# Gate products of the recurrent branch on two row groups of TensorE, with four half-height tanh in place of two

## What is computed

```
xb = x.reshape(B, T, LRU_BLOCKS, LRU_BW)                  # 16 blocks of 64 features
r_gate = sigmoid(einsum('btnc,ncd->btnd', xb, w_r) + b_r)
i_gate = sigmoid(einsum('btnc,ncd->btnd', xb, w_i) + b_i)
log_a  = -8 * r_gate * softplus(-lam_param)
a      = exp(log_a)
u      = sqrt(-expm1(2 * log_a)) * (i_gate * x)
h_t    = a_t * h_(t-1) + u_t                              # a scan over time
```

## Time and profile before

| | |
|---|---|
| median of 3 runs | 2040.4 us (2035.8 to 2043.44) |
| the profiled execution | 2036.35 us, of which the span is 2034.6 us |
| PE busy | 98% of the span |
| DVE, ACT, POOL busy | 52%, 47%, 13% |
| mean granted clock of TensorE | 0.995 |
| chain of work that ended last | 82% PE, 8% ACT, 6% DVE, 2% issue |
| gate products (line 797) | 128 records, 393 ns each |
| gate tanh (line 1307) | 32, of 697 ns (`tr`) and 707 ns (`ti`) |

### The profile page before, as it was taken

One profiled execution on the slowest core, in us unless ns is written; L12 is line 12 of the kernel. 1 busy time (PEld: TensorE's weight loads), 2 busy tenths in 40 slices (PEclk: granted clock), 3 DMA queues, 4 the chain that ended last, 5 costly groups with the idle time before them and its releaser, 6 DMA issues.

```text
span 2034.6 us, 38848 instructions
## 1 busy us (share of the span) xinstructions
PE 1991.7 (98%) x15734; PEld 1944.4 (96%) x15734; DVE 1062.1 (52%) x1976; ACT 955.4 (47%) x1503; POOL 263.5 (13%) x292
## 2 busy tenths in 40 slices
PE   7999999999999999999999999999999999999997
PEld 7999999999998999999989999999999999999997
DVE  5657575755446432343457566767554374224334
ACT  5465656565236431332364757565732454213323
POOL 2312121100111200120021111120001012002100
PEclk9999999999999999999999999999999999999998
DMA  5323232222232323232313232323232323233321
GB/s 135 98 63 102 63 105 68 82 63 83 87 100 64 92 83 93 84 93 84 103 53 98 63 97 67 96 68 87 68 93 83 103 64 93 83 88 89 90 86 66
DMA packets 308456, 172.00 MB, mean 85 GB/s; under 512 B 7593, under 2 KB 303873, under 8 KB 308321
## 3 DMA queue, kind: packets, MB, share of 16 engines
q1 hardware_dynamic: 300768, 155.47, 26.4%
q0 software_dynamic: 7520, 14.59, 2.5%
q10 hardware_dynamic: 32, 0.04, 0.0%
HBM read 158.86 MB, written 11.21 MB: 84 GB/s over the span
## 4 chain that ended last, share of the span: by engine, by line
PE 82%; ACT 8%; DVE 6%; issue 2%; DMA 1%; SPq 0%; ACTq 0%; DVEq 0%
PE PJ L672 65%; PE PJ L684 4%; PE PJ L845 4%; PE PX L873 2%; ACT w_hi L1101 2%; PE PX L684 1%; PE PX L891 1%; DVE w_lo L1576 1%; PE PX L911 1%; DVE T L1687 1%; PE PX L689 1%; PE PX L927 1%; DMA w_raw<-in_w_in 1%; DVE uc L1817 1%; ACT L1318 1%
## 5 line engine op out<-in xcount | busy, mean ns | idle before, releaser
L1576 DVE TENSOR_TENSOR w_lo<-w_raw,w_hi 128x1024 fp32r<-128x1024 f32 x284 | 384.1, 1357 | 368.4 <-ACT w_hi L1101 367.6
L672 PE MATMUL PJ<-h_hi,w_hi 128*128 128x272 f32 x2304 | 490.6, 294 | 2.6 <-DVE T L1687 1.9
L672 PE MATMUL PJ<-h_hi,w_lo 128*128 128x272 f32 x2304 | 475.8, 289 | 0.0
L672 PE MATMUL PJ<-h_lo,w_hi 128*128 128x272 f32 x2304 | 474.6, 288 | 0.0
L1101 ACT ACTIVATE w_hi<-w_raw 128x1024 fp32r<-128x1024 f32 x284 | 297.8, 1051 | 232.9 <-DMA w_raw<-in_w_down 115.6
L672 PEld LDWEIGHTS PJ<-h_hi,w_hi 128*128 128x128 f32 x2304 | 360.2, 189 | 12.8 <-issue 9.5
L672 PEld LDWEIGHTS PJ<-h_lo,w_hi 128*128 128x128 f32 x2304 | 361.4, 189 | 0.0
L672 PEld LDWEIGHTS PJ<-h_hi,w_lo 128*128 128x128 f32 x2304 | 360.4, 189 | 0.0
L672 PE MATMUL PJ<-u_hi,w_hi 128*128 128x272 f32 x960 | 198.4, 288 | 0.0
L672 PE MATMUL PJ<-u_hi,w_lo 128*128 128x272 f32 x960 | 197.4, 288 | 0.0
L672 PE MATMUL PJ<-u_lo,w_hi 128*128 128x272 f32 x960 | 197.1, 287 | 0.0
(11 more groups left out here) (340 smaller groups left out, 3501.8 us busy)
## 6 DMA issues: line engine op xcount, KB each, us to landing
w_raw<-in_w_in SPq DMA_DIRECT2D x110, 512.0 KB, 3.8
w_raw<-in_w_down SPq DMA_DIRECT2D x64, 512.0 KB, 3.8
w_raw<-in_w_up SPq DMA_DIRECT2D x62, 512.0 KB, 4.1
w_raw<-in_w_branch_attn SPq DMA_DIRECT2D x16, 512.0 KB, 3.8
w_raw<-in_w_branch_lru SPq DMA_DIRECT2D x16, 512.0 KB, 3.7
w_raw<-in_w_out SPq DMA_DIRECT2D x16, 512.0 KB, 3.8
out_prompt_k<-stage POOLq DMA_DIRECT2D x16, 256.0 KB, 2.8
out_prompt_v<-GA POOLq DMA_DIRECT2D x8, 512.0 KB, 4.0
```

Source lines behind the costliest of these rows:

```text
L672: mm = pe.matmul(PJ[:, buf, half, 0:HT], w[a], src[b][:, k0 + k, HT * half:HT * half + HT], start=first and k == 0 and a + b == 0, stop=en ...
L1576: dve.tensor_tensor(low(n)[:], raw(n), w_hi[:, n.hi, :, :].bitcast(F32), ALU.subtract).then_inc(w_lo_ready, 1)
```

## The change

`w_gate` shrinks to one 128 x 128 matrix for a half `u`: on partitions 0 to 63 stand `w_rg` and `w_ig` of block 0 side by side, on partitions 64 to 127 `w_ig` and `w_rg` of block 1. A product takes 64 partitions (one block, both gates) and 274 columns; there are still four for a half `u`, and the two blocks are on different row groups of TensorE and write different banks. Of block 1 the two gates come out on each other's partitions. ACT puts them right: four tanh of 64 partitions each, the crossed ones reading partitions 64 to 127 and writing 0 to 63 or the other way round. `w_gate` holds no zeros any more, so the memset and its semaphore go. `tr` is now read from all four banks, so `turn_k(1)` waits for both gates to have been read, and it is moved behind value group 3.

```diff
-        w_gate = sb("w_gate", [P, 2, 2, P])
+        w_gate = sb("w_gate", [P, 2, P])
...
-            pool.memset(w_gate[:], 0.0).then_inc(wg_zero, 1)
...
-                            pool.dma_start(w_gate[64 * b:64 * b + 64, u, j, 64 * b:64 * b + 64],
+                            pool.dma_start(w_gate[64 * b:64 * b + 64, u, 64 * (j ^ b):64 * (j ^ b) + 64],
...
-                for j in range(2):
-                    for half in range(2):
-                        mm = pe.matmul(PX[:, 2 * j + half, 0:LH], w_gate[:, u, j, :], uc[:, LH * half:LH * half + LH], start=True, stop=True)
-                mm.then_inc(gates_done, 1)
+                for half in range(2):
+                    for b in range(2):
+                        rows_ = slice(64 * b, 64 * b + 64)
+                        mm = pe.matmul(PX[:, 2 * b + half, 0:LH], w_gate[rows_, u, :], uc[rows_, LH * half:LH * half + LH], start=True, stop=True)
+                        if half == 1:
+                            mm.then_inc(gates_done, 1)
...
-                    pe.wait_ge(lru_act, 10 * g - 9 + 5 * m)
+                    pe.wait_ge(lru_act, 10 * g - 8 + 5 * m)
...
                     v_groups(l, p, (2,))
-                    turn_k(l, p, 1)
+                    if p == 0:
+                        turn_k(l, p, 1)
                     v_groups(l, p, (3,))
                     if p == 0:
                         turn_past(l, p)
                     else:
+                        turn_k(l, p, 1)
                         sub_ssq(l, p - 1, 1)
...
                 for j, t in enumerate((tr, ti)):
-                    act.activation(t[:].rearrange("p (a b) -> p a b", a=2), PX[:, 2 * j:2 * j + 2, 0:LH], ACT.Tanh, scale=0.5,
-                                   bias=gain(l, f, R_BR + j)).then_inc(lru_act, 1)
+                    for b in range(2):
+                        to, of = slice(64 * b, 64 * b + 64), slice(64 * (j ^ b), 64 * (j ^ b) + 64)
+                        i = act.activation(t[to, :].rearrange("p (a b) -> p a b", a=2), PX[of, 2 * b:2 * b + 2, 0:LH], ACT.Tanh, scale=0.5,
+                                           bias=gain(l, f, R_BR + j)[to, :])
+                    i.then_inc(lru_act, 1)
```

More of the change, by code:

```diff
@@ L243, in hybrid_encoder @@
             sem, ("o_squared", "o_ssq", "o_rs", "o_normed", "o_hi_ready", "o_lo_ready"))
-        wg_zero, wg_landed, hist_ready, conv_first, conv_step, gates_done, lru_act, lru_step = map(
-            sem, ("wg_zero", "wg_landed", "hist_ready", "conv_first", "conv_step", "gates_done", "lru_act", "lru_step"))
+        wg_landed, hist_ready, conv_first, conv_step, gates_done, lru_act, lru_step = map(
+            sem, ("wg_landed", "hist_ready", "conv_first", "conv_step", "gates_done", "lru_act", "lru_step"))
         gelu_done, ga_done, gb_done, l_hi_ready, l_lo_ready, b_scaled, m_hi_ready, m_lo_ready = map(
@@ L548, in load_gate_weights @@
                 g = 4 * l + p
-                need(pool, wg_zero, 1)
-                need(pool, gates_done, 2 * g, first=p == 0)
+                need(pool, gates_done, 4 * g, first=p == 0)
                 own_wait(pool)
@@ L1302, in gate_acts @@
                 f = 2 * p + u
-                act.wait_ge(gates_done, g2 + 1)
+                act.wait_ge(gates_done, 2 * g2 + 2)
                 need(act, lru_step, 12 * g2, first=p + u == 0)
```

## The result

The changed kernel takes 2061.16 us (median of 4 runs, 2059.22 to 2062.49); the kernel before took 2039.33 (median of 4, 2035.8 to 2043.44). The ratio is 1.011 (95% interval 1.0098 to 1.0122): 1.1% slower, 21.8 us. The forecast was 2051 (2043 to 2058). The sign came out, the size was half of it.

The account below looks back on a forecast made before the run. PE, busy 1991.7 of 2034.6 us, was taken as the bound, with ACT's gate work just ahead of it. Pair stages +5.5 and `gate_b` tiles +4.8 gave +10.3 on the median 2040.4: 2051 us, range 2043 to 2058.

Parts of the forecast that it names:

- Which view decides: How far ACT and DVE are ahead of PE where PE asks for them decides, since PE's work goes to ACT.
- PE's gain: At each of sixteen gate places, products on row groups take 1.56 us instead of 1.84, a gain of 0.28.
- All four places: PE held up at value group 1, behind group 3 by `turn_k(1)` (+0.11), at tile 6 (0.91), at `sub_ssq` (2.40).
- the 1.50 us for which ACT stands before `uc`: In a pair's stage ACT stood 1.50 us for DVE's `ti`, so the tanh delay of 1.20 passes on whole.
- four slots, not five: Gate products in the order written were counted as five slots of 0.23 us plus 0.41 for entering and leaving.
- four half-height tanh take 2.40 where two took 1.20: At each gate place, tanh follow 0.60 us apart even at half height, delaying ACT behind them by 1.20.
- 0.70 each, the whole duration without overlap: Upper bound for the half-height tanh at a gate place: a delay of ACT of 1.60 us.
- 0.91: In each of six pair stages, tile 6 waits for `v_rows(1)` and is 0.91 us late, 5.5 us in all.
- The clock: Rival: TensorE's clock falls in the new waits in the `gate_b` tiles, up to 3.1 us more, 2054; chance 0.17.
- expected to start at 163.11: In a pair's stage, PE can start `turn_k(1)` 0.14 us after the fourth tanh ends at 162.97.
- Costed at nothing: The `w_gate` weight loads and the memset cost nothing; the `k2` store, about 2.4 to 3 us later, delays no score.
- 0.05 us dearer: A tanh 0.05 us dearer or cheaper moves each of eight stages by 0.40 us, 3.2 in all.

Follow-up runs that it names:

- experiment 2: The kernel before with each full-height tanh split into two of 64 partitions, nothing crossed: 2068.97 us against 2038.2, ratio 1.0154.

## Why the prediction was wrong, step by step

- **Which view decides.** Right: PE's gain never reached the end, ACT's chain did. All four places and the engines waited for came as named, and the 1.50 us for which ACT stands before `uc` was there unchanged.
- **PE's gain.** Taken as 1.56 us a gate place, measured 1.24: four slots, not five. Blocks on different row groups overlap wholly, and 0.3 us is the price of entering and leaving. It was hidden in either case, so no harm came of it. The page "TensorEngine Tiling (Array Packing)" of the Trainium skill, section Theoretical Speedup, has up to twice the speed at 64. The trace stays within that: 1.24 of 1.84, with the price in it.
- **The step that failed is a term of the sum, the time of the four tanh: "four half-height tanh take 2.40 where two took 1.20", with "0.70 each, the whole duration without overlap" as the upper bound.** The first half of the argument, that half height costs full time, held; the second, that they would follow at 0.60 as before, did not. They took 2.91, or 1.71 more than two where the sum had 1.20, and over the bound of 1.60 even, since behind a change of half ACT also stands 0.01 to 0.03 us. With 0.73 the prediction's own steps give 6 x (0.91 + 2 x 0.51) = 11.6 in the stages (measured 11.8) and 2 x 3.42 = 6.8 behind the pairs (measured 6.2, as PE's gain counts there): 18.4 in place of 10.3. The Trainium skill's page "ScalarE: Activation LUTs", section What ACT_TABLE_LOAD costs, states that back-to-back ACTIVATEs overlap by about 93 ns. The traces agree where two start on the same partition (0.60 of 0.70) and disagree where they don't (0.71 to 0.74).
- **The clock.** The rival was named with its place and cause, at a chance of 0.17 and 3.1 us at most. It came in both traces and both layers, with 5.5 us in the first: the wait was 3.7 and not 2.9, and the stretch at the lower level longer than the one it was priced from. That the fall would come was not certain: the waits of 3.0 us in experiment 2 brought none. With 18.4 + 3.1 the rival's time would have been 2062.
- **`turn_k(1)`** was expected to start at 163.11 and started, in that frame, at 162.94 + 1.06 = 164.00: 0.9 later, by the same term. Costed at nothing, and seen to wait for nothing: the weight loads, the memset, the later store of k2.

The range failed at its upper end: it allowed a tanh to be 0.05 us dearer, and each came 0.13 dearer (0.73 for 0.60). A row with two ACTIVATEs that start on different partitions would have settled it, but the kernel before had none: every one that I measured 0.60 or 0.10 from starts on partition 0.

## What to carry to other kernels

Before splitting an elementwise instruction over partition halves, count what it adds in the slot of its engine, start to start: on ACT two tanh of half the height cost 1.46 us where one whole cost 0.60, whichever way they are crossed. A gain on the busiest engine is worth nothing where another engine's chain stands just ahead of it; there, first move what hangs on the chain (a buffer's emptying, a sum that shares a bank), then take the gain. And a long wait of TensorE costs more than its length when the clock falls behind it.

## What the runs showed of the hardware

- In these traces an ACTIVATE overlapped the next by about 0.10 us where both read from the same first partition and wrote to the same first partition, and not where either changed: tanh of 548 columns follow at 0.59 to 0.62 us in the first case and at 0.71 to 0.74 in the second, for a duration of 0.69 to 0.72. The height doesn't matter: a full-height one overlaps with one on partitions 0 to 63 (16 of 16 places) and not with one on 64 to 127 (0 of 16). Reading from one half and writing to the other by itself costs nothing more (2.91 us for four, crossed or not).
- fp32 products of 64 partitions on two row groups run two at a time although each goes in two passes: 1.24 us for four, entering and leaving included, against 1.84 for four at full height.
- The wait of 3.7 us of PE was followed by the clock's lower level in six of six cases (three traces, two layers each); in the first trace that cost 2.6 and 2.9 us more. Waits at the same place of 2.4 us were followed by it in two of two cases, waits of 3.0 us in another kernel in none of two.
